# Attention scores of the second block's mixers as stacked split products on the full array

## What is computed

```python
q = apply_partial_rope(split_heads(q), cos, sin)
k = apply_partial_rope(split_heads(k), cos, sin)
s = einsum('qd,kd->qk', q, k) * 64 ** -0.5     # float32, per head
# dilated: masks of three window patterns, softmax of each, combined
# differential: softmax(q1 k1') - lam * softmax(q2 k2') per pair of heads, then @ v
```

## Time and profile before

| | us |
|---|---|
| median of 3 runs | 3098.12 (3095.55 to 3100.03) |
| the profiled execution | 3099.16 |
| its span | 3097.0 |
| PE busy | 3032.2 (98%) |
| DVE busy | 1762.7 (57%) |
| ACT busy | 1247.9 (40%) |
| POOL busy | 297.5 (10%) |

### The profile page before, as it was taken

One profiled execution on the slowest core, in us unless ns is written; L12 is line 12 of the kernel. 1 busy time (PEld: TensorE's weight loads), 2 busy tenths in 40 slices (PEclk: granted clock), 3 DMA queues, 4 the chain that ended last, 5 costly groups with the idle time before them and its releaser, 6 DMA issues.

```text
span 3097.0 us, 37956 instructions
## 1 busy us (share of the span) xinstructions
PE 3032.2 (98%) x15004; PEld 2408.1 (78%) x15004; DVE 1762.7 (57%) x2584; ACT 1247.9 (40%) x2068; POOL 297.5 (10%) x257
## 2 busy tenths in 40 slices
PE   7999999999999999999999999999999999999998
PEld 6777888887777888887667878888866688788886
DVE  7765644357666544467775635344577755354444
ACT  6644323245554322344444534232344444342322
POOL 2011100011011100011011102000110011020001
PEclk9999999999999999999999999999999999999999
DMA  4111333332112233332112322333221133123332
GB/s 139 55 49 62 94 98 95 95 96 81 55 48 67 94 99 99 95 95 74 55 55 89 123 69 82 96 100 98 89 61 56 48 96 115 62 89 98 100 95 82
DMA packets 79872, 259.16 MB, mean 84 GB/s; under 512 B 8021, under 2 KB 18393, under 8 KB 79321
## 3 DMA queue, kind: packets, MB, share of 16 engines
q1 hardware_dynamic: 78968, 252.99, 26.3%
q0 software_dynamic: 736, 3.87, 0.4%
HBM read 254.73 MB, written 2.10 MB: 83 GB/s over the span
## 4 chain that ended last, share of the span: by engine, by line
PE 82%; DVE 7%; issue 6%; DVEq 1%; POOLq 1%; ACT 1%; DMA 0%; POOL 0%; ACTq 0%
PE bank L572 67%; PE bank L502 2%; PE bank L1132 1%; DVE w_lo L2192 1%; POOLq L3081 1%; PE bank L798 1%; PE bank L1143 1%; PE bank L1345 1%; PE bank L1364 1%; PE bank L1301 1%; PE bank L1087 1%; PE bank L1153 1%; PE bank L1157 1%; PE bank L764 1%; PE bank L828 0%
## 5 line engine op out<-in xcount | busy, mean ns | idle before, releaser
L572 PE MATMUL bank<-a_hi,w_hi 128*128 128x512 f32 x2120 | 848.1, 400 | 20.3 <-DVE w_lo L2192 16.3
L572 PE MATMUL bank<-a_hi,w_lo 128*128 128x512 f32 x2120 | 828.5, 391 | 0.0
L572 PE MATMUL bank<-a_lo,w_hi 128*128 128x512 f32 x2120 | 827.5, 390 | 0.0
L2192 DVE TENSOR_TENSOR w_lo<-w_raw,w_hi 128x1024 fp32r<-128x1024 f32 (+1 forms) x474 | 611.1, 1290 | 282.5 <-ACT w_hi L1468 280.7
L1468 ACT ACTIVATE w_hi<-w_raw 128x1024 fp32r<-128x1024 f32 (+1 forms) x474 | 494.9, 1045 | 427.2 <-DMA w_raw<-weights 427.0
L572 PE MATMUL bank<-b_hi,w_hi 128*128 128x512 f32 (+1 forms) x1388 | 536.3, 386 | 1.8 <-DVE w_lo L2192 0.6
L572 PE MATMUL bank<-b_lo,w_hi 128*128 128x512 f32 (+1 forms) x1388 | 528.1, 381 | 0.0
L572 PE MATMUL bank<-b_hi,w_lo 128*128 128x512 f32 (+1 forms) x1388 | 528.0, 380 | 0.0
L572 PEld LDWEIGHTS bank<-a_hi,w_hi 128*128 128x128 f32 x2120 | 399.8, 189 | 122.1 <-issue 22.4
L572 PEld LDWEIGHTS bank<-a_hi,w_lo 128*128 128x128 f32 x2120 | 399.2, 188 | 85.4
L572 PEld LDWEIGHTS bank<-a_lo,w_hi 128*128 128x128 f32 x2120 | 399.9, 189 | 82.6 <-issue 3.3
(11 more groups left out here) (344 smaller groups left out, 3272.3 us busy)
## 6 DMA issues: line engine op xcount, KB each, us to landing
w_raw<-weights SPq DMA_DIRECT2D x458, 512.0 KB, 3.5
w_raw<-weights SPq DMA_DIRECT2D x16, 384.0 KB, 3.0
x<-x SPq DMA_DIRECT2D x8, 256.0 KB, 7.2
mem<-mem POOLq DMA_DIRECT2D x2, 1024.0 KB, 5.2
out<-x SPq DMA_DIRECT2D x8, 256.0 KB, 2.1
mem<-mem SPq DMA_DIRECT2D x1, 1024.0 KB, 12.0
ple<-ple POOLq DMA_DIRECT2D x2, 512.0 KB, 4.2
o<-c_level SPq DMA_DIRECT2D x1, 512.0 KB
```

The source lines that it names most:

```text
L572: last = mm(bank[unit_bank(u) if at is None else at][:, 0:cols], w[:, u % SLOTS, ks], t[:, k, 0:cols], start=(k == begun and n == 0), stop ...
L2192: tt(w_lo[:, u % SLOTS, w], w_raw[:, u % SLOTS, w], f32(w_hi[:, u % SLOTS, w]), ALU.subtract).then_inc(w_lo_ready, 1)
```

## The change

For pairs 1 to 7 a query is kept in two fp32r parts stacked in 128 rows: for head e the high part on the head's own 64 partitions, the low part on the other 64 (`f_q`). The key's high part stands on both halves (`f_k` high), and its low part on the head's own half with zeros on the other (`f_k` low). Two products per head, on all 128 rows, give (q_hi + q_lo) k_hi + q_hi k_lo. Pair 0 keeps the float32 product. ACT makes the high parts (two casts for the query, four for the key), DVE the low ones (two subtractions each), and clears the zero halves once per layer. Queries and keys now lie in four y tiles, two for each parity of the pair (`raw`), which frees the room for the parts. `score(p, 0)` waits for the key parts of its pair. On DVE `rope_add(r, 1)` moves ahead of `ahead(first + 3 * r + 4)`. POOL's only edit is the tile's place.

```diff
--- before.py
+++ after.py
@@ -234,6 +234,8 @@
         y = place("y", [P, 24, S])
         p_hi, p_lo = place("p_hi", [P, 2, S], F32R, at_y), place("p_lo", [P, 2, S], F32R, at_y + 4 * KB)
         at_o, at_v = region(16 * KB), region(16 * KB)
+        f_q = place("f_q", [P, 2, 2, S], F32R, at_y + 8 * KB)
+        f_k = tuple(place(name, [P, 2, 2, S], F32R, at_y + kb * KB) for name, kb in (("f_k_hi", 16), ("f_k_lo", 24)))
         o = place("o", [P, DT, S], F32, at_o)
         v = place("v", [P, ST, D], F32, at_v)
 
@@ -367,6 +369,7 @@
         lam_made, lam_summed, lam_exp = sem("lam_made"), sem("lam_summed"), sem("lam_exp")
         f_scored, f_max, f_exp, f_norm, f_turned, f_copied = (
             sem("f_scored"), sem("f_max"), sem("f_exp"), sem("f_norm"), sem("f_turned"), sem("f_copied"))
+        f_hi, f_key, f_split = sem("f_hi"), sem("f_key"), sem("f_split")
         f_out, f_taken, f_rot, f_sin, f_cos, f_roped, f_valued, f_v_ready = (
             sem("f_out"), sem("f_taken"), sem("f_rot"), sem("f_sin"), sem("f_cos"), sem("f_roped"),
             sem("f_valued"), sem("f_v_ready"))
@@ -396,6 +399,10 @@
             return t[64 * e:64 * e + 64]
 
         OUT_ORDER = (0, 1, 4, 6, 5, 7, 2, 3)
+
+        def raw(r, k):
+
+            return y[:, 2 * k + r % 2, :]
 
         def score_banks(l, s):
 
@@ -1122,15 +1129,22 @@
 
                 def score(p, q):
                     n = steps + 4 * p + q
-                    if q == 0:
-                        pe.wait_ge(f_roped, 2 * (pairs + p + 1))
-                        if p == 0:
-                            pe.wait_ge(bank_free, first + 3)
+                    if q == 0 and p == 0:
+                        pe.wait_ge(f_roped, 2 * (pairs + 1))
+                        pe.wait_ge(bank_free, first + 3)
+                    elif q == 0:
+                        pe.wait_ge(f_key, (PAIRS - 1) * l + p)
+                        pe.wait_ge(f_split, (PAIRS - 1) * l + p)
                     if n > 0:
                         pe.wait_ge(f_exp, 2 * n)
                     for e in range(2):
-                        mm(bank[F_S[e]][:, :], half_of(y[:, p, qs(q)], e), half_of(y[:, 8 + p, :], e),
-                           start=True, stop=True).then_inc(f_scored, 1)
+                        if p == 0:
+                            last = mm(bank[F_S[e]][:, :], half_of(raw(0, 0)[:, qs(q)], e), half_of(raw(0, 1), e), start=True, stop=True)
+                        else:
+                            for i in range(2):
+                                last = mm(bank[F_S[e]][:, :], f_q[:, p % 2, e, qs(q)], f_k[i][:, p % 2, e, :],
+                                          start=(i == 0), stop=(i == 1))
+                        last.then_inc(f_scored, 1)
 
                 def turn(p, q):
                     n = steps + 4 * p + q
@@ -2008,6 +2022,21 @@
                     act.wait_ge(n_summed, p + 1)
                     f(g_r[:, 32 + ST * p:32 + ST * p + ST], bank[F_O][:, 0:ST], ACT.Copy)
 
+                def query_high(r):
+                    act.wait_ge(f_roped, 2 * (pairs + r) + 1)
+                    for e in range(2):
+                        last = f(half_of(f_q[:, r % 2, e, :], e), half_of(raw(r, 0), e), ACT.Copy)
+                    last.then_inc(f_hi, 1)
+
+                def key_high(r):
+                    act.wait_ge(f_roped, 2 * (pairs + r) + 2)
+                    for e in range(2):
+                        last = f(half_of(f_k[0][:, r % 2, e, :], e), half_of(raw(r, 1), e), ACT.Copy)
+                    last.then_inc(f_hi, 1)
+                    for e in range(2):
+                        last = f(half_of(f_k[0][:, r % 2, e, :], 1 - e), half_of(raw(r, 1), e), ACT.Copy)
+                    last.then_inc(f_key, 1)
+
                 def values(r):
                     act.wait_ge(f_valued, pairs + r + 1)
                     f(v[:, :, qs(r)], bank[F_R][:, :].rearrange("p (a b) -> p a b", a=ST), ACT.Copy).then_inc(f_v_ready, 1)
@@ -2022,6 +2051,8 @@
                 for r in range(1, PAIRS + 1):
                     last = r == PAIRS
                     ahead(first + 3 * r + 2 if not last else first + 3 * r + 1)
+                    if r > 1:
+                        key_high(r - 1)
                     exps(r - 1, 0)
                     if not last:
                         ahead(first + 3 * r + 3)
@@ -2040,6 +2071,8 @@
                         out_rounded((2, 3))
                     values(r - 1)
                     copies(r - 1, 2)
+                    if not last:
+                        query_high(r)
                     if diff and 2 <= r < PAIRS:
                         tile_sums_kept(r - 2)
                     if last:
@@ -2781,7 +2814,7 @@
                 def evict(r, k):
                     u = c.unit
                     dve.wait_ge(unit_done, u + 1)
-                    b, t = bank[pair_bank(first, u)], y[:, 8 * k + r, :]
+                    b, t = bank[pair_bank(first, u)], raw(r, k) if k < 2 else y[:, 16 + r, :]
                     if k == 0:
                         stt(t, b[:, :], 0.125, r_x[:, :], ALU.mult, ALU.mult).then_inc(bank_free, 1)
                     else:
@@ -2824,15 +2857,28 @@
                     if k == 1 and r > 0:
                         dve.wait_ge(f_v_ready, pairs + r)
                     dve.drain()
-                    dve.stream_shuffle(bank[F_R][:, :], y[:, 8 * k + r, :], ROPE_SWAP).then_inc(f_rot, 1)
+                    dve.stream_shuffle(bank[F_R][:, :], raw(r, k), ROPE_SWAP).then_inc(f_rot, 1)
                     dve.drain()
                     tt(f_t[:, k, :], bank[F_R][:, :], sin_t[:, :], ALU.mult).then_inc(f_sin, 1)
 
                 def rope_add(r, k):
                     dve.wait_ge(f_cos, 2 * (pairs + r) + k + 1)
                     dve.wait_ge(f_sin, 2 * (pairs + r) + k + 1)
-                    t = y[:, 8 * k + r, :]
+                    t = raw(r, k)
                     tt(t, t, f_t[:, k, :], ALU.add).then_inc(f_roped, 1)
+
+                def query_low(r):
+                    dve.wait_ge(f_hi, 2 * ((PAIRS - 1) * l + r) - 1)
+                    for e in range(2):
+                        t = f_q[:, r % 2, e, :]
+                        tt(half_of(t, 1 - e), half_of(raw(r, 0), e), f32(half_of(t, e)), ALU.subtract)
+
+                def key_low(r):
+                    dve.wait_ge(f_hi, 2 * ((PAIRS - 1) * l + r))
+                    for e in range(2):
+                        hi, lo = (half_of(t[:, r % 2, e, :], e) for t in f_k)
+                        last = tt(lo, half_of(raw(r, 1), e), f32(hi), ALU.subtract)
+                    last.then_inc(f_split, 1)
 
                 cut = 1.8446743e19
 
@@ -2861,6 +2907,8 @@
                 ahead(first + 2)
                 recip_of_columns(r_x, X_SUM_BANK if l else SUM_BANK)
                 ahead(first + 3)
+                for e in range(2):
+                    dve.memset(f32(half_of(f_k[1], 1 - e)[:, :, e, :]), 0.0)
                 evict(0, 0)
                 evict(0, 1)
                 rope_sin(0, 0)
@@ -2910,9 +2958,11 @@
                     normalise(r - 1, 3)
                     if more:
                         rope_sin(r, 1)
+                        query_low(r)
+                        rope_add(r, 1)
                         ahead(first + 3 * r + 4)
-                        rope_add(r, 1)
                         evict(r, 2)
+                        key_low(r)
                     else:
                         out_low((2, 3))
                 if diff:
```

## The result

The changed kernel takes **3109.29 us** (median of 7 runs, 3107.23 to 3112.09), the kernel before on the same chip 3099.46 us: a ratio of 1.0037 with a 95% interval of 1.0027 to 1.0046. It is slower, by about 10 us, where the forecast was 5.9 us more, 3104.0 us and "no change". The profiled execution took 3111.28 us, 2.0 above its median; its span is 3109.5 us against 3097.0. Of all executions in this document one was slow, 11,587.22 us at a mean granted clock of 0.563 (one of the four of experiment 10), and no ratio counts it.

The account below looks back on a forecast made before the run. PE, busy for 98% of the span, was taken to bound the kernel. The terms -5.0 + 0.7 + 1.95 + 2.5 + 4.6 + 1.2 = +5.9 us gave a median of 3104.0 us, "no change", range 3095 to 3110.

Parts of the forecast that it names:

- What bounds: Whole kernel: PE, busy for 98% of the span, so gains must be PE time; DVE work costs where PE waits.
- PE's share: Score steps: four fp32r products replace two float32 ones; a step gains 0.23 us, one ahead of outputs 0.15.
- At most 0.84: Upper limit of PE's gain per pair from its scores: 3 x 0.23 + 0.15 = 0.84 us.
- the rule: Trainium skill: 64-row PE tiles run in parallel; had they run serially, 56 changed steps would gain some 50 us more.
- The chain, "6.07 us in all": DVE, key's sine product to split keys, 6.07 us; six dilated pairs -5.0 us, six differential pairs +0.12 each, +0.7.
- a chain 0.5 us longer than 6.07: Dilated pairs, part of the slower rival (chance 0.40): 6 x 0.5 = 3.0 us, 3105.9 without any fall.
- The last pairs: PE waits for split keys ahead of score(7, 0): 2.6 us dilated, costing +1.95; 3.5 us differential, costing +2.5.
- The memsets: DVE's opening chain: two per layer at 1.14 us each add in full, +4.6 us (3.0 at the lower bound).
- The clock, "I count one fall there": One fall of the granted clock behind the differential last pair's 3.5 us wait, partly over idle time: +1.2 us.
- Slower: the clock: Rival: full clock falls over work behind both last-pair waits, 4.75 + 3.4 = +8.15 us in all, 3106.3; chance 0.40.
- Cheap passes: Rival: 64-row operations cost half, so the chain and memsets shrink: -4.65 us, 3093.5; chance 0.14.
- the change doesn't do what it says: Rival: the stacked PE products run at two passes each, like float32: +45 us over 56 steps; chance 0.04.

Follow-up runs that it names:

- experiment 10: Changed kernel with an unread 128x512 DVE product added behind the two query subtractions: 3119.42 us, ratio 1.0067.
- experiments 9: Changed kernel with a third, unread 64x512 DVE subtraction added behind the two query subtractions: 3120.06 us, ratio 1.0070.
- experiment 6: Changed kernel with DVE's key rope addition and key subtractions ahead of the value eviction, and the zeroes written by POOL: 3089.64 us, ratio 0.9975.
- experiment 4: Changed kernel with 6 (dilated) and 8 (differential) unused PE products in the wait ahead of the last pair's first score: 3105.52 us, ratio 1.0026.
- experiment 1: Changed kernel with both memsets of each layer moved from DVE to POOL, behind its first two cosine products: 3104.44 us, ratio 1.0023.
- experiment 5: Changed kernel with DVE's key rope addition and key subtractions moved ahead of the value eviction: 3095.7 us, ratio 0.9988.
- experiments 3: Changed kernel with 10 (dilated) and 14 (differential) unused PE products in the wait ahead of the last pair's first score: 3108.94 us, ratio 1.0034.
- experiment 2: Changed kernel with pair 7 kept on float32 scores, without casts and subtractions: 3100.88 us, ratio 1.0008.

## Why the prediction was wrong, step by step

**What bounds.** Right: the gain had to be PE time, and DVE's position in time decided. In every steady pair of the changed kernel PE waits for the same chain (experiments 9 and 10).

**PE's share.** Four products at 0.23 us and 0.15 us for the first score are as measured (experiment 6). The step "4 x 0.23 + 0.24 = 1.15 us, so a step gains 0.23 us" looked only ahead of the transposes. Timeline of PE, changed kernel, dilated layer:

```profile
1549.33 0.39 PE L579 MATMUL bank<-a_hi,w_lo 128*128 128x512 f32 x1
...
1550.46 1.03 PE L1157 MATMUL bank<-small,prob 128*128 128x128 f32 x8
```

That is 1.13 us, and about 0.06 more comes back behind the transposes (0.79 us from their start to the next weight product instead of 0.85), so three scores give 0.9 instead of 0.69. "At most 0.84" should have been 1.09, 1.5 us more over six dilated pairs. That two 64-row products run side by side was right: nothing of the 50 us that the rule would have given is in any run.

**The chain, "6.07 us in all".** This is the step that failed first and cost most. It measured 6.35 and 6.36. The two query subtractions start 0.11 us late and take 1.81 with their wait for POOL instead of 1.74, and the key subtractions 1.38 up to the end of the second instead of 1.30, since starts of these pairs lie 0.69 apart and not 0.61. With "no margin to speak of" in the dilated layer, the 0.28 came out as a wait of 0.26 and a slower first product: 1.09 shrank to 0.70 (2.3 us over six pairs), so six pairs gave 4.2 instead of 5.0. In the differential layer +0.12 became +0.38, about the 0.28 again: +2.3 instead of +0.7. The rival named this, "a chain 0.5 us longer than 6.07"; 0.3 was enough.

**The last pairs.** Waits of 2.6 and 3.5 us were forecast. Counted in the prediction's way 3.0 and 3.8 came (the rows' 2.85 and 3.66 count from the end of the product before): the 0.28 of the chain in both, and in the dilated layer the 0.15 us by which DVE was to run ahead of PE and did not (5.84 us lie between the sine product and the last weight product before, 5.86 now). Their price is 2.25 and 2.77 (experiment 4) against 1.95 and 2.5. Right, and short by about what the chain was short.

**The memsets.** +4.6 forecast, 4.5 by the sine products, 4.6 by the marks of experiment 1. Right, and for a reason that was only half seen: the operation takes 0.91 us, and 0.25 us of issuing brings it to 1.16. The estimate by the Trainium skill (VectorE: DVE Perf Modes, Zero memsets can be issued as uint32), 1.07 us each, lies above the operation (0.91) and below what it costs DVE (1.16); for the sum the measured 1.16 decides.

**The clock, "I count one fall there".** This is the largest miss of a single term. Both last pairs had a fall in the profile, 3.4 and 6.8 us long, which cost 1.67 and 2.98; with the 0.9 given back behind the mixer it is +3.75 against +1.2. The forecast took one fall of 1.7 us with a part "over idle time" off. It was the fall of the earlier trace rows that lay partly over idle time and cost 0.9, while the float32 outputs behind the two waits are all PE work, as the rival *Slower: the clock* said. Nothing in the rows before could tell how many falls would come, and experiment 1's profile has one less.

Together, on top of 5.9: +2.3 and +1.6 for the chain in the pairs, +0.6 for the two waits, -1.5 for the scores' larger gain, +2.55 for the clock and -0.1 for the memsets, 5.45 us, which is the profile's 11.3. The scores' gain (1.5 us too small) and the chain's cost in the dilated layer (2.3 too small) hid each other in part, so that its pairs came out near the forecast by luck. The medians' 9.8 is 1.5 less; a fall that some executions lack would account for it, but that isn't shown. The rival with the longer chain, "8.15 + 3 = 11", is what came, and held the upper end of the range. *Cheap passes* and *the change doesn't do what it says* found nothing for them.

## What to carry to other kernels

Price a split that feeds PE by the whole chain from its first input to the semaphore, and where that chain meets PE without margin, let its error bars, not its central value, set the forecast: here 0.28 us of chain became 4.5 us over fourteen pairs. Before a change is judged, put the new instructions in the order of who waits for them, and the constants on an engine that idles: the same arithmetic went from 3109.29 to 3089.64 us. Where a loop's last round has less work to hide behind than the others, let it keep the old form: that gave the last 4.0 us, to 3085.64.

## What the runs showed of the hardware

- The same bare wait of 3.66 us was followed by 6.8 us at a lower granted clock in the changed kernel, and by none in experiment 1. Shorter ones were followed by a fall too: 2.83 to 2.85 us in three profiles of three, 2.23 us in one of two (experiment 5, not 6). With unused products in the wait the clock stayed at 2.4 GHz in both layers in experiments 3 and 4.
- A fall behind a wait costs about half its length (1.67 of 3.4 us, 2.98 of 6.8) where the work behind it is all PE's: 8 outputs of 128x512 went from 3.70 to 5.75 us. The fall of 3.4 us behind the mixer, where PE waits in between, cost about 0.9: 34 us behind the last output copy DVE is 0.86 to 0.90 us ahead of the kernel before in six of the seven profiles without it (0.56 in experiment 2), and within 0.07 us of it in the four others that have it.
- A 64x512 operation takes what a 128x512 one takes: 0.684 and 0.692 us on DVE at the same place. Two on different halves of the partitions start 0.69 us apart (the key subtractions), where a 128x512 one frees the engine after 0.61 (1566.36 to 1566.97).
- A memset of 64x1,024 float32 elements took 0.91 us on DVE with 0.25 us of issuing between two, and 1.0 us on POOL (two in 2.02 us).
- The row's releaser can be the wrong one of two: ACT was named for PE's waits ahead of the last pairs, and its last cast (L2037) ended 0.4 us before DVE's subtraction did (1626.08 against 1626.51, 2470.72 against 2471.16).
